# First attention of a two-layer stack on one core: keys and values as three-part products, heads paired across groups, query and output products between the pairs

## The chip, the core and the metric

The kernel runs on one core of a Trainium2 chip. The time is device time of one execution in microseconds (us). The engines are TensorE (PE; its weight loads are listed as PEld), VectorE (DVE), ScalarE (ACT), GpSimd (POOL) and SyncE (SP), which here only issues transfers.

## The reference

The model takes 16 meta tokens and 256 tokens of width 1024 through a pooling layer with a feed-forward network, then an attention layer with another one, and then through a second stack (gated branches and 32 routed experts), which the change leaves alone. What is touched is the first attention: 16 query heads of 64 in two groups of 8, each group with one key and value head, and a sliding window over blocks of 128.

```python
kv_in = rms_norm(hs, kv_norm)
k = (kv_in @ w_k + b_k).reshape(B, L, N_KV_HEADS, HEAD_DIM)
v = (kv_in @ w_v + b_v).reshape(B, L, N_KV_HEADS, HEAD_DIM)
...
q = (h @ w_q + b_q).reshape(B, L, N_KV_HEADS, GROUP, HEAD_DIM)
...
logits = jnp.einsum('bnqhgd,bnshd->bhgnqs', q, k_blk,
                    preferred_element_type=jnp.float32) * (HEAD_DIM ** -0.5)
...
m = jnp.maximum(logits.max(axis=-1, keepdims=True), sink)
p = jnp.exp(logits - m)
denom = p.sum(axis=-1, keepdims=True) + jnp.exp(sink - m)
probs = (p / denom).astype(v_blk.dtype)
o = jnp.einsum('bhgnqs,bnshd->bnqhgd', probs, v_blk)
...
return o @ w_o + b_o
```

## The kernel before

**Weights.** SP loads all weights of the dense layers in the order of `STREAM` (L55) into a ring of three slots. Tile number t goes to slot t % 3 and waits until the tile three places back is used up (`tile_done`, L310). For most weights that is when DVE has made the low part of both halves; for `w_kv`, which is not split, it is when the last product with it is done (`kv_psum` at 3). `w_kv` is tile 20, `w_q` 21 and 22, `w_o` 23 and 24, so the first tile of `w_o` follows `w_kv` in slot 2. SP works strictly in order.

**Three-part products.** A weight piece of 2048 columns is split into a rounded part (`wh`, by ACT, `split_hi`, L660) and a rest (`wl`, by DVE, `split_lo`, L668); activations likewise (`xh`, `xl`). A product is then three matmuls in a reduced 32-bit format (`mm3`, L1195): high with high, low with high, high with low. There are two buffers for split pieces and a third one for chosen pieces (`THIRD_FIRST`); a piece waits until the product of the piece before it in its buffer is done.

**First attention, before.** PE makes query columns 0 to 3 (L1233, L1239), then 4 to 7 (L1245, 24 matmuls each), turns the row of scales (L1250), and multiplies keys and values with plain 32-bit matmuls on `mix`, which POOL has filled (L598): keys twice, once for each group, laid out double so that both heads of a pair find them in their half of the partitions (L1258), and values by token (L1263). Then it waits for keys and values (L1266), and goes through 8 pairs of neighbouring heads: `scores`, `turn` (transposes of the weights) and `outputs` (L1301), with the scores two pairs ahead. After the last pair come the 8 output columns of `w_o`, 24 matmuls each. DVE, in its own fixed order, evicts query columns (L1880, L1881) with splits of `w_q` and `w_o` in between (the table `low` hangs the first piece of `w_o` behind query column 4), then keys (L1892) and values (L1899); per pair it adds the bias and takes the maximum (`logits`, L1912 to L1922), normalises (`shares`, L1929 to L1933) and makes the low part of the output (L1938). ACT does the exponentials (L811), the copies of what was turned (L821) and the high part (L826).

The bias table (`brev`) is loaded by SP after the first feed-forward network (L457), ahead of `w_o`.

## Time and profile before

| | us |
|---|---|
| three runs | 1093.58, 1090.06, 1093.87 |
| median | 1093.58 |
| span of the profiled execution | 1091.4 |
| PE busy in it | 980.6 |
| DVE, ACT, POOL busy | 535.7, 410.0, 167.7 |

The page gives the span, first to last instruction; the median of the runs is 2.2 us above it. The chain that ended last lies on PE for 84% of the span and on DVE for 7%; 1% is one transfer of `w_o`. Matmuls are pipelined, so a group's busy time overstates what each takes of the path; the distance between starts is the better price.

### The profile page before, as it was taken

The numbers are of one execution on the slowest core, as the hardware profiler recorded it, in microseconds if no ns is written. First come the engines' busy times: TensorE is split into PE (matmuls) and PEld (weight loads), VectorE is DVE, ScalarE is ACT, GpSimd is POOL, SyncE is SP. The second block draws the span as 40 slices with busy tenths as digits, with TensorE's granted clock in tenths as the row PEclk, the third lists the DMA queues.
The fourth block names the chain that finished last, engine by engine and source line by source line (L and its number), as shares of the span: only waits on it lengthen the run. The fifth ranks groups of instructions, "written<-read, shape, count | busy, mean of one in ns | idle before, by whom it ended". The sixth has DMA issues, their size and how long they took to land.

```text
span 1091.4 us, 16836 instructions
## 1 busy us (share of the span) xinstructions
PE 980.6 (90%) x6809; PEld 822.9 (75%) x6809; DVE 535.7 (49%) x976; ACT 410.0 (38%) x684; POOL 167.7 (15%) x224
## 2 busy tenths in 40 slices
PE   3799999998849999999987999979889999999866
PEld 2599999998737899999987999759644554455365
DVE  4655454347165655554435538674523334333254
ACT  3533333445047743344444456633211111111153
POOL 5432323015000333332101000000100000000000
PEclk8899999999959999999997999779799999999979
DMA  7325434454060425453562431028269999999601
GB/s 284 154 91 204 169 130 156 163 189 154 28 279 4 154 97 212 154 182 132 187 232 78 160 116 55 34 92 366 97 239 420 418 418 407 409 409 419 259 1 38
DMA packets 25646, 212.51 MB, mean 195 GB/s; under 512 B 2001, under 2 KB 5345, under 8 KB 5729
## 3 DMA queue, kind: packets, MB, share of 16 engines
q1 hardware_dynamic: 25568, 211.43, 50.0%
q8 instruction: 55, 0.90, 0.3%
q14 instruction: 23, 0.18, 0.0%
HBM read 210.35 MB, written 1.07 MB: 194 GB/s over the span
## 4 chain that ended last, share of the span: by engine, by line
PE 84%; DVE 7%; ACT 3%; issue 2%; POOL 2%; DMA 1%; POOLq 0%; DVEq 0%; ACTq 0%
PE ps L1195 48%; PE ps L1557 10%; PE ps L1571 5%; PE ps L1186 3%; PE ps L1580 3%; PE ps L1126 2%; PE ps L1529 2%; PE ps L1530 1%; DVE wl L668 1%; DVE mix L1685 1%; PE ps L1233 1%; DMA ring<-in_w_o 1%; PE ps L1134 1%; PE ps L1515 1%; PE ps L1258 1%
## 5 line engine op out<-in xcount | busy, mean ns | idle before, releaser
L668 DVE TENSOR_TENSOR wl<-ring,wh 128x2048 fp32r<-128x2048 f32 (+2 forms) x106 | 214.8, 2027 | 226.0 <-ACT wh L660 226.0
L660 ACT ACTIVATE wh<-ring 128x2048 fp32r<-128x2048 f32 (+2 forms) x106 | 179.6, 1697 | 304.1 <-PE ps L1195 268.6
L1195 PE MATMUL ps<-xh,wh 128*128 128x256 f32 (+3 forms) x712 | 203.5, 286 | 7.0 <-DVE xl L2227 7.0
L1195 PE MATMUL ps<-xh,wl 128*128 128x256 f32 (+3 forms) x712 | 201.9, 284 | 0.0
L1195 PE MATMUL ps<-xl,wh 128*128 128x256 f32 (+3 forms) x712 | 201.6, 283 | 0.0
L1195 PEld LDWEIGHTS ps<-xh,wh 128*128 128x128 f32 (+3 forms) x712 | 132.9, 187 | 8.5 <-issue 8.1
L1195 PEld LDWEIGHTS ps<-xh,wl 128*128 128x128 f32 (+3 forms) x712 | 132.9, 187 | 0.2
L1195 PEld LDWEIGHTS ps<-xl,wh 128*128 128x128 f32 (+3 forms) x712 | 132.8, 187 | 0.0
L1195 PE MATMUL ps<-acth,wh 128*128 128x272 f32 (+1 forms) x352 | 101.1, 287 | 0.0
L1195 PE MATMUL ps<-actl,wh 128*128 128x272 f32 (+1 forms) x352 | 100.0, 284 | 0.0
L1195 PE MATMUL ps<-acth,wl 128*128 128x272 f32 (+1 forms) x352 | 100.0, 284 | 0.0
L1195 PE MATMUL ps<-xhT,wl 128*128 128x272 f32 x320 | 92.6, 289 | 0.0
L1195 PE MATMUL ps<-xlT,wh 128*128 128x272 f32 x320 | 92.2, 288 | 0.0
L1195 PE MATMUL ps<-xhT,wh 128*128 128x272 f32 x320 | 91.3, 285 | 0.0
L530 POOL TENSOR_TENSOR sq<-sq 128x256 f32<-128x256 f32 (+1 forms) x15 | 20.9, 1397 | 445.7 <-ACT sq L644 445.7
L1195 PEld LDWEIGHTS ps<-acth,wh 128*128 128x128 f32 x352 | 66.5, 189 | 0.2
L1195 PEld LDWEIGHTS ps<-acth,wl 128*128 128x128 f32 x352 | 66.1, 188 | 0.2
L1195 PEld LDWEIGHTS ps<-actl,wh 128*128 128x128 f32 x352 | 66.2, 188 | 0.0
L2211 DVE TENSOR_TENSOR yl<-ps,yh 128x512 fp32r<-128x512 f32 x32 | 20.6, 686 | 91.4 <-ACT yh L1064 91.4
L539 POOL TENSOR_TENSOR mix<-mix 128x272 f32<-128x272 f32 (+1 forms) x44 | 36.7, 835 | 158.5 <-DVE mix L1719 142.6
L1557 PE MATMUL ps<-wring,xb_even 128*64 128x512 f32 x256 | 56.5, 593 | 5.0 <-issue 5.0
L1195 PEld LDWEIGHTS ps<-xhT,wh 128*128 128x128 f32 x320 | 60.4, 189 | 0.0
(382 smaller groups left out, 1778.5 us busy)
## 6 DMA issues: line engine op xcount, KB each, us to landing
wring<-in_w_eg SPq DMA_DIRECT2D x32, 2048.0 KB, 12.5
ring<-in_w_gu SPq DMA_DIRECT2D x22, 2048.0 KB, 8.0
wring<-in_w_ed SPq DMA_DIRECT2D x16, 2048.0 KB, 10.6
ring<-in_w_dn SPq DMA_DIRECT2D x16, 1408.0 KB, 5.9
ring<-in_w_z SPq DMA_DIRECT2D x7, 2048.0 KB, 7.7
ring<-in_w_out SPq DMA_DIRECT2D x4, 1152.0 KB, 5.1
ring<-in_w_q SPq DMA_DIRECT2D x2, 2048.0 KB, 7.7
ring<-in_w_o SPq DMA_DIRECT2D x2, 2048.0 KB, 10.1
```

Of the source, the lines that this page charges most:

```text
L530: pool.tensor_tensor(even, even, odd, ALU.add).then_inc(sem("sq_paired"), 1)
L539: pool.tensor_tensor(mix[:, 6 + j, 0:n], mix[:, 2 + j, 0:n], mix[:, 4 + j, 0:n], ALU.mult)\
L660: act.activation(high[:, 0:size], ring[:, slot, j * size:(j + 1) * size], ACT.Copy)\
L668: dve.tensor_tensor(low[:, 0:size], ring[:, slot, j * size:(j + 1) * size], high[:, 0:size].bitcast(F32), ALU.subtract).then_inc(sem("lo_d ...
L1126: pe.matmul(ps[:, 2 * j + g, 0:n], w[:, k * 256 + g * P:k * 256 + g * P + P], xa[:, k, 0:n], start=(k == 0 and part == 0), stop=False)
L1186: mm(ps[:, 6, 0:n], ones[0:rows, :], square_at(name, c + 1 - chunks)[0:rows, 0:n], start=(c < chunks), stop=(c == last))\
L1195: ins = mm(o, p, q, start=first and n == 0, stop=last and n == 2)
L1529: mm(out, h2h[:, k, at], select[:, k, :], start=(k == 0), stop=False)
L1557: ins = mm(ps[rows, 4, :], x[:, k, rows], chunk(b, c)[:, j, i * 512:(i + 1) * 512], start=(k == 0), stop=(k == KD - 1))
L1571: ins = mm(ps[rows, 6 + i, :], heT[:, k, rows], chunk(b, GU_CHUNKS)[:, j, k * D + i * 512:k * D + (i + 1) * 512], start=(k == 0), stop=(k ...
L1580: ins = mm(ps[:, c // 2, c % 2 * SEQ:(c % 2 + 1) * SEQ], y[:, c * P:(c + 1) * P], weights, start=False, stop=last and y is parts[-1], skip ...
L2211: dve.tensor_tensor(yl[:, i * 512:(i + 1) * 512], ps[:, 6 + i, :], yh[:, i * 512:(i + 1) * 512].bitcast(F32), ALU.subtract).then_inc(sem(" ...
```

## The change

`w_kv` leaves the ring. It is loaded early, right after the last tile of the first gate and up weights, into the free end of slot 2 (columns 4096 to 6143), only one copy of the keys and the values, in two transfers of 128 columns by 8 rows of each partition. It becomes a piece of its own in the order of splits, between the two tiles of `w_q`. `w_q` and `w_o` are tiles 20 to 23 now; each is loaded in four transfers that bring head u and head u+8 next to each other, so a pair is one head of each group and finds keys and values of its group in its half of the partitions. ACT and DVE make `xkh` and `xkl` in place of POOL's product; keys and values (as rows by channel) are three-part products, and the values are turned by three transposes. DVE evicts query columns 4 to 7 inside the loop over pairs. On PE, query column 4 stands ahead of the loop, 5 to 7 in its first three rounds, and the output products of columns 0 and 1 (`project`) in its last four. The outputs go to `att_h` and `att_l` instead of `xh` and `xl`, so that queries can still be made. The two score blocks of one head share a PSUM bank and stand one after the other; DVE goes by head as well. Later on, because every ring tile behind `w_kv` moves by one slot, the first loads of the experts go to slots 0, 1, 2, 3 instead of 1, 2, 3, 0, behind `w_out` tiles 1, 2, 2, 3, and the two tiles of `w_ple` are waited for at earlier counts. Two semaphores of the router are merged.

```diff
-STREAM = [("w_pool", 1, 2048), ("w_gu0", NF // 2, 4096), ("w_dn0", KD, FF), ("w_kv", 1, 3072),
+STREAM = [("w_pool", 1, 2048), ("w_gu0", NF // 2, 4096), ("w_dn0", KD, FF),
...
+SPLIT = [(_name, _p) for _name, _n, _ in STREAM if _name != "w_pool" for _p in range(2 * _n)]
+SPLIT.insert(SPLIT.index(("w_q", 2)), ("w_kv", 0))
+NUMBER = {_piece: _i for _i, _piece in enumerate(SPLIT)}
...
-        THIRD_FIRST = ("w_gu0", "w_q", "w_gu1", "w_z")
+        THIRD = (("w_gu0", 0), ("w_q", 0), ("w_q", 2), ("w_o", 1), ("w_gu1", 0), ("w_z", 0))
...
+                    if name == "w_q":
+                        src = a["w_q"][half, :, i * PIECE:(i + 1) * PIECE].rearrange("p (k c n) -> p k c n", k=KD, c=2)
+                        dst = ring[:, slot, 0:2 * PIECE].rearrange("p (c k h n) -> p h k c n", c=2, k=KD, h=2)
+                        for c in range(2):
+                            sp_.dma_start(dst[:, half, :, c, :], src[:, :, c, :]).then_inc(done, 16)
+                        continue
+                    for odd in range(2):
+                        src = a["w_o"][i, odd * HD:(odd + 1) * HD, :].rearrange("p (c h n) -> p c h n", c=2, h=2)
+                        dst = ring[half * HD:(half + 1) * HD, slot, 0:2 * PIECE].rearrange("p (c o n) -> p c o n", c=2, o=2)
+                        sp_.dma_start(dst[:, :, odd, :], src[:, :, half, :]).then_inc(done, 16)
...
+            kv = a["w_kv"].rearrange("a p (k n) -> (a p) k n", n=3 * P)
+            for j in range(2):
+                sp_.dma_start(wkv.rearrange("p (k n) -> p k n", n=2 * P)[:, :, j * P:(j + 1) * P],
+                              kv[:, :, HD + j * 3 * HD:HD + j * 3 * HD + P]).then_inc(sem("kv_loaded"), 16)
...
-            pool.wait_ge(sem("delta_ready"), 2 * KD)
-            for c in range(KD):
-                wait_hs(pool, 1, c)
-                pool.tensor_scalar(mix[:, c, :], hs[:, c, :], V("kv_norm", c), None, ALU.mult).then_inc(sem("kvin_ready"), 1)
...
-            split_hi(act, "w_q", *halves("w_q", 1, PIECE)[0])
+            kv_hi(act)
+            for c in range(KD):
+                act.activation(xkh[:, c, :], hs[:, c, :], ACT.Copy, scale=V("kv_norm", c)).then_inc(sem("xkh_ready"), 1)
             rsqrt(act, chain, "pre1", D, T)
-            split_hi(act, "w_q", *halves("w_q", 1, PIECE)[1])
-            for x in halves("w_o", 0, PIECE):
-                split_hi(act, "w_o", *x)
+            for x in halves("w_q", 1, PIECE):
+                split_hi(act, "w_q", *x)
+            split_hi(act, "w_o", *halves("w_o", 0, PIECE)[0])
...
+                if u in (1, 4):
+                    split_hi(act, "w_o", *(halves("w_o", 0, PIECE)[1] if u == 1 else halves("w_o", 1, PIECE)[0]))
             attended_high(HEAD_PAIRS - 1)
-            for k in range(NB):
-                split_hi(act, "w_o", *halves("w_o", 1, PIECE)[k])
-                for c in range(2 * k, 2 * k + 2):
-                    wo_out(act, c)
-            split_hi(act, "w_gu1", *halves("w_gu1", 0, PIECE)[0])
-            for c in range(4, KD):
+            for c in range(KD):
+                if c == 2:
+                    split_hi(act, "w_o", *halves("w_o", 1, PIECE)[1])
+                if c in (4, 6):
+                    split_hi(act, "w_gu1", *halves("w_gu1", 0, PIECE)[c // 2 - 2])
...
-            for c in range(4, KD):
-                pe.wait_ge(sem("lo_done"), FIRST_PIECE["w_q"] + c // 2 + 1)
-                pe.wait_ge(sem("q_ready"), c - 3)
-                for k in range(KD):
-                    ins = mm3(ps[:, c % 4, 0:SEQ], q_weights(c, k), (xh[:, k, 0:SEQ], xl[:, k, 0:SEQ]), k == 0, k == KD - 1)
-                ins.then_inc(sem("q_psum"), 1)
-            pe.wait_ge(sem("r_ready"), NORM["pre1"] + 1)
-            for j in range(NB + 1):
-                cols = slice(0, P) if j == 0 else slice(N_META + (j - 1) * P, N_META + j * P)
-                ins = pe.transpose(ps[:, 5, j * P:(j + 1) * P], r_of("pre1")[:, cols], ident)
-            ins.then_inc(sem("rcol_psum"), 1)
-            slot, rnd = tile_at(FIRST["w_kv"])
-            pe.wait_ge(sem(f"tile_ready{slot}"), 16 * (rnd + 1))
-            wkv = ring[:, slot, 0:3072].rearrange("p (k n) -> p k n", k=KD)
+            kvh, kvl = split_buffer("w_kv", 0, 0)
+            pe.wait_ge(sem("lo_done"), NUMBER["w_kv", 0] + 1)
             for j in range(2):
                 for k in range(KD):
-                    pe.wait_ge(sem("kvin_ready"), k + 1)
-                    ins = mm(ps[:, 4 + 3 * j, 0:T], wkv[:, k, j * P:(j + 1) * P], mix[:, k, :], start=(k == 0), stop=(k == KD - 1))
+                    pe.wait_ge(sem("xk_ready"), k + 1)
+                    at = slice(k * 2 * P + j * P, k * 2 * P + (j + 1) * P)
+                    ins = mm3(ps[:, 4 + j, 0:T], (kvh[:, at], kvl[:, at]), (xkh[:, k, :], xkl[:, k, :]), k == 0, k == KD - 1)
...
+            def query(c):
+
+                pe.wait_ge(sem("lo_done"), NUMBER["w_q", c // 2] + 1)
+                pe.wait_ge(sem("q_ready"), 4 if c < 6 else c - 1)
                 for k in range(KD):
-                    ins = mm(ps[0:cols.stop - cols.start, 6, j * P:(j + 1) * P], mix[:, k, cols], wkv[:, k, 2 * P:3 * P],
-                             start=(k == 0), stop=(k == KD - 1))
-            ins.then_inc(sem("kv_psum"), 1)
-            pe.wait_ge(sem("kT_ready"), 2)
-            pe.wait_ge(sem("v_ready"), NB + 1)
+                    ins = mm3(ps[:, 2 + c % 2, 0:SEQ], q_weights(c, k), (xh[:, k, 0:SEQ], xl[:, k, 0:SEQ]), k == 0, k == KD - 1)
...
             def scores(u):
-                for t in range(4):
-                    h, b = 2 * u + t % 2, t // 2
-                    rows = slice(t % 2 * HD, t % 2 * HD + HD)
-                    first, n = keys_of(t)
+                if u >= 4:
+                    pe.wait_ge(sem("q_ready"), u + 1)
+                for j in range(2):
+                    rows = slice(j * HD, j * HD + HD)
                     if u:
-                        pe.wait_ge(sem("lg_ready"), 4 * (u - 1) + t + 1)
-                    mm(ps[:, t, 0:n], qT[rows, u, b * P:(b + 1) * P], kT[rows, h // 8, first:first + n],
-                       start=True, stop=True).then_inc(sem("s_psum"), 1)
+                        pe.wait_ge(sem("lg_ready"), 4 * (u - 1) + 2 * j + 2)
+                    for t in (j, 2 + j):
+                        first, n = keys_of(t)
+                        ins = mm(score_bank(t)[:, 0:n], qT[rows, u, t // 2 * P:(t // 2 + 1) * P], kT[rows, first:first + n],
+                                 start=True, stop=True)
+                    ins.then_inc(sem("s_psum"), 1)
...
+            def project(c, k):
+
+                if k == 0:
+                    pe.wait_ge(sem("lo_done"), NUMBER["w_o", c // 2] + 1)
+                pe.wait_ge(sem("o_ready"), k + 1)
+                first = (k % 2 * 4 + k // 2) * 256 + c % 2 * P
+                at = slice(first, first + P)
+                return mm3(wo_bank(c), [x[:, at] for x in split_buffer("w_o", c // 4, c // 2 % 2)],
+                           (att_h[:, k, :], att_l[:, k, :]), k == 0, k == KD - 1)
+
+            pe.wait_ge(sem("kv_ready"), 1)
             scores(0)
             scores(1)
+            query(4)
+            values()
+            pe.wait_ge(sem("v_ready"), 2)
             for u in range(HEAD_PAIRS):
+                if u < 3:
+                    query(5 + u)
                 if u + 2 < HEAD_PAIRS:
                     scores(u + 2)
+                if u >= 4:
+                    for c in range(2):
+                        project(c, u - 4)
                 turn(u)
                 if u:
                     outputs(u - 1)
+            for k in range(4, 6):
+                for c in range(2):
+                    project(c, k)
             outputs(HEAD_PAIRS - 1)
-            for c in range(KD):
-                piece = FIRST_PIECE["w_o"] + c // 2
-                pe.wait_ge(sem("lo_done"), piece + 1)
-                if c >= 4:
-                    pe.wait_ge(sem("sq_ready"), SQ0["mixpost1"] + c - 3)
+            for c in range(2, 4):
+                for k in range(6):
+                    project(c, k)
+            for c in range(4):
+                for k in range(6, KD):
+                    ins = project(c, k)
+                ins.then_inc(sem("wo_psum"), 1)
+            for c in range(2):
+                sum_squares("mixpost1", c, SEQ)
+            for c in range(4, KD):
+                pe.wait_ge(sem("sq_ready"), SQ0["mixpost1"] + c - 3)
                 for k in range(KD):
-                    pe.wait_ge(sem("o_ready"), k + 1)
-                    at = slice(k * 256 + c % 2 * P, k * 256 + c % 2 * P + P)
-                    ins = mm3(ps[:, c % 4, 0:SEQ], [x[:, at] for x in split_buffer("w_o", c // 4, c // 2 % 2)],
-                              (xh[:, k, 0:SEQ], xl[:, k, 0:SEQ]), k == 0, k == KD - 1)
+                    ins = project(c, k)
                 ins.then_inc(sem("wo_psum"), 1)
-                if c >= 2:
-                    sum_squares("mixpost1", c - 2, SEQ)
+                sum_squares("mixpost1", c - 2, SEQ)
...
-            split_lo(dve, "w_q", *halves("w_q", 1, PIECE)[0])
+            kv_lo(dve)
+            for c in range(KD):
+                dve.wait_ge(sem("xkh_ready"), c + 1)
+                dve.scalar_tensor_tensor(xkl[:, c, :], hs[:, c, :], V("kv_norm", c), xkh[:, c, :].bitcast(F32),
+                                         ALU.mult, ALU.subtract).then_inc(sem("xk_ready"), 1)
...
-            low = {1: ("w_q", halves("w_q", 1, PIECE)[1]), 4: ("w_o", halves("w_o", 0, PIECE)[0])}
-            for c in range(KD):
...
+            def keyed():
+
+                dve.wait_ge(sem("kv_psum"), 1)
+                chain(dve.tensor_tensor(sq[:, 2, :], ps[:, 4, 0:T], r, ALU.mult))
+                dve.tensor_scalar(kT, sq[:, 2, :], key_bias, None, ALU.add).then_inc(sem("kv_ready"), 1)
+
+            def valued():
+
+                dve.wait_ge(sem("kv_psum"), 2)
+                dve.tensor_tensor(vT, ps[:, 5, 0:T], r, ALU.mult).then_inc(sem("kv_ready"), 1)
+
+            def by_token():
+
+                dve.wait_ge(sem("kv_psum"), 3)
+                b_v = R("b_v", P)
+                dve.tensor_tensor(vtok[0:N_META, 0, :], ps[0:N_META, 7, 0:P], b_v[0:N_META, :], ALU.add).then_inc(sem("v_ready"), 1)
+                dve.tensor_tensor(vtok[:, 1:NB + 1, :], ps[:, 7, P:3 * P].rearrange("p (b n) -> p b n", b=NB),
+                                  b_v.unsqueeze(1).to_broadcast([P, NB, P]), ALU.add).then_inc(sem("v_ready"), 1)
+
+            queried(0)
+            queried(1)
+            split_lo(dve, "w_q", *halves("w_q", 1, PIECE)[0])
+            queried(2)
+            queried(3)
+            keyed()
+            split_lo(dve, "w_q", *halves("w_q", 1, PIECE)[1])
             dve.wait_ge(sem("tables_loaded"), 64)
-            dve.wait_ge(sem("kv_psum"), 3)
-            b_v = R("b_v", P)
-            for j in range(NB + 1):
-                rows = slice(0, N_META if j == 0 else P)
-                dve.scalar_tensor_tensor(vtok[rows, j, :], ps[rows, 6, j * P:(j + 1) * P], small[rows, 128 + j:129 + j], b_v[rows, :],
-                                         ALU.mult, ALU.add).then_inc(sem("v_ready"), 1)
...
             logits(0)
+            valued()
             logits(1)
-            split_lo(dve, "w_o", *halves("w_o", 0, PIECE)[1])
+            by_token()
             for u in range(HEAD_PAIRS):
                 shares(u)
+                if u < 4:
+                    queried(4 + u)
                 if u + 2 < HEAD_PAIRS:
                     logits(u + 2)
                 if u >= 2:
                     attended_low(u - 2)
+                if u in (2, 3, 5):
+                    split_lo(dve, "w_o", *[*halves("w_o", 0, PIECE), halves("w_o", 1, PIECE)[0]][(2, 3, 5).index(u)])
             for u in range(HEAD_PAIRS - 2, HEAD_PAIRS):
                 attended_low(u)
-            for x in halves("w_o", 1, PIECE):
-                split_lo(dve, "w_o", *x)
+            split_lo(dve, "w_o", *halves("w_o", 1, PIECE)[1])
```

On SP, between the first feed-forward weights and the second ones, before:

```order
L424 DMA ring<-in_w_gu 128x4096 x2
L424 DMA ring<-in_w_dn 128x2816 x8
L424 DMA ring<-in_w_kv 128x3072
L424 DMA ring<-in_w_q 128x4096 x2
L457 DMA work<-bias_rows 128x16x256
L424 DMA ring<-in_w_o 128x4096 x2
```

and now:

```order
L461 DMA ring<-in_w_gu 128x4096 x2
L489 DMA ring<-in_w_kv 128x8x128 x2
L494 DMA small<-in_vec 64x4 x4
L461 DMA ring<-in_w_dn 128x2816 x8
L441 DMA ring<-in_w_q 128x8x128 x8
L502 DMA work<-bias_rows 128x16x256
L446 DMA ring<-in_w_o 64x2x1024 x8
```

The load of `w_kv` moved ahead of eight tiles; `w_o` still follows the bias table (`bias_rows`).

On DVE, from the low part of the query input to the first maximum of the scores (L1912 before, L2024 now, shown as ISA), before. The marks stand for further evictions of query columns and for the first piece of `w_o` among them:

```order
L1871 SCALAR_TENSOR_TENSOR xl<-hs,vec,xh 128x256 x8
L668 TENSOR_TENSOR wl<-ring,wh 128x2048
L1880 TENSOR_TENSOR sq<-ps,rstd 128x256
L1881 TENSOR_SCALAR work<-sq,vec 128x2x128
...
L668 TENSOR_TENSOR wl<-ring,wh 128x2048
...
L1892 TENSOR_TENSOR sq<-ps,rstd 128x272
L1893 TENSOR_SCALAR work<-sq,vec 128x272
...
L1899 SCALAR_TENSOR_TENSOR work<-ps,small,row 128x128 x2
L1912 ISA work,small<-ps,work 128x144
```

and now:

```order
L1968 SCALAR_TENSOR_TENSOR xl<-hs,vec,xh 128x256 x8
L733 TENSOR_TENSOR wl<-ring,wh 128x2048
L1973 SCALAR_TENSOR_TENSOR xkl<-hs,vec,xkh 128x272 x8
L1981 TENSOR_TENSOR sq<-ps,rstd 128x256
...
L720 TENSOR_TENSOR third_l<-ring,third_h 128x8x128 x2
...
L1989 TENSOR_TENSOR sq<-ps,rstd 128x272
L1990 TENSOR_SCALAR work<-sq,small 128x272
L720 TENSOR_TENSOR wl<-ring,wh 128x8x128 x2
L2024 ISA work,small<-ps,work 128x144
```

Before the first scores stand two splits of `w_q` and the one of `w_kv`, and none of `w_o`; the values (L1995) come behind the first pair's maxima.

On PE, from the last query column to the first scores, before:

```order
L1195 MATMUL ps<-xl,wh 128x256
L1250 MATMUL ps<-cst,rstd 128x128 x3
L1258 MATMUL ps<-mix,ring 128x272 x16
L1263 MATMUL ps<-ring,mix 16x128 x8
L1263 MATMUL ps<-ring,mix 128x128 x16
L1276 MATMUL ps<-work 128x144 x2
L1276 MATMUL ps<-work 128x256 x2
```

and now, from the last rest product of query column 3 (L1312) to the first query column between the pairs:

```order
L1312 MATMUL ps<-xl,wh 128x256 x16
L1268 MATMUL ps<-xkh,wh 128x272
L1268 MATMUL ps<-xkh,wl 128x272
L1268 MATMUL ps<-xkl,wh 128x272
...
L1348 MATMUL ps<-work 128x144
L1348 MATMUL ps<-work 128x256
L1348 MATMUL ps<-work 128x144
...
L1268 MATMUL ps<-xh,third_h 128x256
L1268 MATMUL ps<-xh,third_l 128x256
L1268 MATMUL ps<-xl,third_h 128x256
```

The scores stand directly behind 16 groups of three matmuls for keys and values, and the query columns 4 to 7 behind the scores.

## Rows read from the trace of the kernel before

**Rows 1.** The chain that ended last, in order of time: start, duration, what.

```profile
271.95 11.39 PE ps L1195 x96
283.67 7.33 PE ps L1258 x32
291.00 5.63 PE ps L1263 x48
296.65 7.82 DMA ring<-in_w_o
...
346.88 11.58 PE ps L1195 x96
...
371.65 0.71 PE ps L1186 x2
```

**Rows 2.** DVE in order of time, 259 to 313: start, duration, instruction, [idle before].

```profile
259.60 4.47 DVE L1871 SCALAR_TENSOR_TENSOR xl<-hs,vec,xh 128x256 fp32r<-128x256 f32 x8
263.99 2.28 DVE L668 TENSOR_TENSOR wl<-ring,wh 128x2048 fp32r<-128x2048 f32 x1
...
306.44 2.29 DVE L668 TENSOR_TENSOR wl<-ring,wh 128x2048 fp32r<-128x2048 f32 x1 [28.05 <-ACT wh L660]
308.65 0.42 DVE L1880 TENSOR_TENSOR sq<-ps,rstd 128x256 f32<-128x256 f32 x1
...
310.81 0.28 DVE L1888 COPY small<-ps 128x1 f32<-128x1 f32 x3
```

**Rows 3.** ACT in the same order, 268 to 308.

```profile
304.50 3.71 ACT L660 ACTIVATE wh<-ring 128x2048 fp32r<-128x2048 f32 x2 [30.59 <-DMA ring<-in_w_o]
```

**Rows 4.** SP's issues of transfers, 215 to 345.

```profile
227.94 0.33 SPq L424 DMA_DIRECT2D ring<-in_w_kv  x1
236.68 8.61 SPq L424 DMA_DIRECT2D ring<-in_w_q  x2
250.68 0.38 SPq L457 DMA_DIRECT2D work<-bias_rows  x1
296.65 0.81 SPq L424 DMA_DIRECT2D ring<-in_w_o  x2
```

**Rows 5.** PE in order of time, first pairs of heads.

```profile
313.57 5.49 PE L1276 MATMUL ps<-work 64*128 64x144 f32 x24 [16.95 <-DVE work L1899]
...
325.03 0.34 PE L1287 MATMUL ps<-cst,work 128*128 128x128 f32 x1
...
326.06 1.24 PE L1301 MATMUL ps<-mix,work 16*64 16x128 f32 x16
327.23 0.95 PE L1276 MATMUL ps<-work 64*128 64x144 f32 x8
```

**Rows 6.** DVE in order of time, inside the loop over pairs.

```profile
316.44 0.30 DVE L1912 CUSTOM_DVE_ANT_0 work<-ps,work 128x144 f32<-128x144 f32 x1
...
318.18 2.29 DVE L668 TENSOR_TENSOR wl<-ring,wh 128x2048 fp32r<-128x2048 f32 x1
...
330.24 1.03 DVE L1933 TENSOR_SCALAR work<-work,small 128x144 f32<-128x144 f32 x4
...
333.52 1.02 DVE L1933 TENSOR_SCALAR work<-work,small 128x144 f32<-128x144 f32 x4
```

**Rows 7.** POOL's sum of two squares behind the output products.

```profile
356.32 1.39 POOL L530 TENSOR_TENSOR sq<-sq 128x256 f32<-128x256 f32 x1 [85.47 <-ACT sq L644]
```

**Rows 8.** Stretches: length, busy PE, PEld, DVE, ACT, POOL, PE clock, DMA share, GB/s.

```profile
256.00:260.00 4.00, 3.95 (x20) 3.95 (x21) 3.93 (x9) 3.59 (x10) 2.17 (x3) 0.57 0.50 160
...
301.00:305.00 4.00, 0.00 (x0) 0.00 (x0) 0.00 (x0) 0.50 (x1) 0.00 (x0) 0.50 1.01 430
...
321.00:325.00 4.00, 3.40 (x16) 2.56 (x16) 3.86 (x24) 1.99 (x7) 0.00 (x0) 0.52 0.90 291
325.00:329.00 4.00, 4.00 (x42) 3.10 (x40) 3.69 (x22) 3.69 (x15) 0.00 (x0) 1.00 0.57 240
...
337.00:341.00 4.00, 2.84 (x31) 1.85 (x28) 3.86 (x22) 3.95 (x17) 0.00 (x0) 1.00 0.01 2
```

**Rows 9.** Transfers: KB each, median us from issue to landing.

```profile
ring<-in_w_q SPq DMA_DIRECT2D x2, 2048.0 KB, 7.7
...
work<-bias_rows SPq DMA_DIRECT2D x1, 2048.0 KB, 8.0
```

186 lines of the change are left out of this document (113 added, 73 removed).

## The prediction, made before the result was known

> **What bounds the kernel now.** I read the chain that ended last first, between 270 and 373 us, where the change lies. PE makes query columns 4 to 7 from 271.95 in 96 matmuls (11.39 us), then keys and values until 296.65; then the chain leaves PE for 7.82 us of a transfer of `w_o` [rows 1]. The orders of the other engines say why. SP issues `w_o` at 296.65, just when the last product with `w_kv` ends, since both use slot 2 [rows 4]. ACT has stood 30.59 us waiting for it [rows 3], DVE 28.05 us for ACT [rows 2], with the evictions of three query columns, keys and values behind that split. PE starts its scores at 313.57 after 16.95 us without work [rows 5], and at half clock: the granted clock is 0.50, that is 1.2 GHz, from 301, and at 1.00, 2.4 GHz, only from about 325 [rows 8]. In the loop over pairs PE is at 2.84 of 4 us busy while DVE has 3.86 [rows 8]: DVE sets the pace there, 3.28 us per pair (330.24 to 333.52) [rows 6]. From 346.88 PE is alone on the chain again, until the last sum of squares ends at 371.65 + 0.71 = 372.36 [rows 1]. Everything later follows that moment, so I compute the new time of it.
>
> **Prices.** A three-part matmul on 256 columns: 11.39 / 96 = 0.119 us, a group of three 0.357, a query column 2.85 [rows 1]; on 272 columns 0.119 x 272/256 = 0.126. An eviction of a query column on DVE: (310.81 - 308.65) / 3 = 0.72. A split of 2048 columns 2.29, a low part of a 256-column input 4.47 / 8 = 0.56, so 0.59 at 272 [rows 2]. `logits` of one pair: 318.18 - 316.44 = 1.74; the pace of 3.28 less these leaves 1.5 for `shares` and the low part, which I take as 1.3 and 0.33 (some 0.1 is given back by overlap) [rows 6]. `turn`: 326.06 - 325.03 = 1.03, of which I take 0.9 between other work; `outputs` 327.23 - 326.06 = 1.17 [rows 5].
>
> Scores of a pair take 0.95 us for 8 records, four of 144 and four of 256 columns [rows 5]. Keys show a plain 32-bit matmul of 272 columns at 7.33 / 32 = 0.229 us a record [rows 1]; at that rate 1600 columns are 1.35 us. So before, where the two heads (two halves of the partitions) alternate, they overlap. Now both blocks of one head stand together. I take 1.3 us, near the serial end, and 0.95 as the other bound: over three pairs on PE's path that is 1 us. The Trainium skill, TensorEngine Tiling (Array Packing), section Tiling Modes, says that different tiles of rows can load and multiply in parallel; the 0.95 us agree, and by it the new order loses what the old one had. By that rule alone the sum would be as mine; without it 1 us less.
>
> **Part by part.** Start: PE at 271.95, as before.
>
> 1. Keys and values: 48 x 0.126 = 6.0 us in place of 13.3, from the end of the query columns at 271.95 + 11.39 = 283.34 to 296.65 [rows 1]; PE is through at 278.0. DVE must have the low parts: it is free at 263.99, one split (2.3) and 8 x 0.59 bring it to 271.0, just ahead of PE's start and always ahead of its groups. ACT's extra 8 copies and one split fit into time in which it waits. POOL loses its 8 products, on nobody's path.
>
> 2. Before the first scores DVE has four query columns (2.9), two splits of `w_q`, each now two instructions on halves (2.4 each, my estimate from 2.29), and the keys (0.75): 271.0 + 8.5 = 279.5. PE has issued scores(0) by 279.3 and waits for the first head's maximum; scores(1) end near 281.5. Query column 4 to 284.4, three transposes (0.45) to 284.8; DVE adds the bias to the values by 285.5, so PE enters the loop at 285.6. The two waits cost 1.7 us in all.
>
> 3. Rounds 0 to 2 are PE's: a query column 2.85, scores 1.3, turn 0.9, in two of them outputs 1.17: 5.05 + 6.2 + 6.2 brings PE to 303.1. This is where three of four query columns are paid; they hide the DVE work of these rounds, not the other way round.
>
> 4. From there DVE sets the end again, since it now has query column 7 and three splits of `w_o` in the loop. Scores(4) end at 301.1, after the query column and the scores of round 2; the rest of their `logits`, a low part and the first split take it to 304.8; round 3 without that: 1.3 + 0.72 + 1.74 + 0.33 + 2.29 = 6.4; round 4: 3.4; round 5: 5.7; shares of round 6: 1.3. That is 321.6. PE has 2.6 us idle at most at a time, and its 8 groups of `w_o` in rounds 4 to 7 hide there.
>
> 5. The tail is PE's: half a turn 0.45, outputs 1.17, two groups 0.7, turn 0.9, outputs 1.17, four groups 1.4, outputs 1.17 = 7.0, to 328.6. Then 64 - 12 = 52 groups of `w_o` at 0.357 = 18.6, to 347.2. Sums of squares, 1.6. One new wait: the sums of columns 0 and 1 are queued ahead of column 4 and need two evictions on ACT and POOL's sum of 1.39 [rows 7], which start only when column 1 is closed, two columns earlier: 1.1 us. The last evictions, 0.7 us. Together 350.7; I say 351.
>
> The gain is 372.4 - 351 = 21.4 us. By terms: the stall 16.95, keys and values 7.3, some 7 of the 11.4 us of query columns hidden, the slow clock at the start of the loop some 3, 12 of 64 groups hidden (4.3); against that two waits (2.8), scores (some 1 on PE's path), and the splits and evictions which now lengthen the loop on DVE, some 13, where before they stood under the stall.
>
> **Transfers.** `w_q` goes from one transfer to four, of runs of 512 bytes. Its first tile now takes the place of `w_kv` at 227.94 [rows 4]. Its two splits take some 4.5 us, and PE is at work on the query columns by 256 (3.95 of 4 us busy [rows 8]), so the tile may take until 250: 22 us for 2048 KB. The bias table, also 2048 KB and in runs of 1 KB, took 8.0 us [rows 9]. Even half that rate, 16 us, is hidden. `w_o` is issued at about 251 behind the bias table and is wanted at 278; both tiles and the table are 6 MB, at 430 GB/s [rows 8] 15 us. Cost 0, bounds 0 and 10 us (a quarter of the rate for `w_q`). Later on, the new order of expert slots and the earlier `w_ple` change no wait that I find on the chain, 0.
>
> **Rivals.** (a) The clock. It fell to 0.50 in 301 to 305, after 4 us of idle PE, and averaged 0.57 in 256 to 260; it stayed at 1.00 with PE busy 2.84 of 4 us [rows 8]. My rounds 3 to 6 have PE busy about 60%, with pauses of 2.6 us, nearer to the latter. If it falls once and takes as long to come back as before (313.6 to 325), 11.4 us of PE's work run at half speed: 5.7 us, time 1078. (b) The slower side: the clock stays at 1.2 GHz through the whole loop, because no stretch is busy enough. Then queries too cost double: 11.4 more, and turns, scores, outputs and groups, some 30 us of work, take 60, of which DVE's time covers 10. That is 32 us over my figure, 1104. It decides at 43 us of half clock on PE's path, where the gain is gone. Against it: the query columns are dense. (c) The stall stays in another form: a piece of `w_o` or `w_q` comes late, to ACT first, and everything behind it in its fixed order waits. Only keys, values and hidden groups are gained, 7 to 10 us: 1084. (d) More: scores overlap as before, DVE's splits find cover, the two waits vanish: 4 us more, 1068.
>
> **How the numbers follow.** The profiled span of 1091.4 becomes 1070.0; the median stands 2.2 us above that span, so 1093.6 - 21.4 = 1072.2, and I say 1072. Chances: forecast (1069 to 1076) 0.64, (a) 0.15, (d) 0.11, (c) 0.06, (b) 0.04. The range from 1065 to 1083 takes in (d), with 3 us for the spread of the runs (1090.06 to 1093.87), and (a); it leaves out (b), (c) and the worst of the splits. About 0.5%, 5.5 us, is what a measurement of this kernel can tell from no change. Faster by more than that: 0.94; within: 0.03; slower: 0.03.
>
> **What would show it.** Right: `w_o` issued near 251, no idle time of ACT on it, no PE pause over 3 us between 272 and 351, keys and values in 6 us, PE paused before turns in rounds 3 to 6 with DVE as releaser, the clock at 1.00 throughout, the last sum of squares near 351 and everything later 21 us earlier with unchanged distances. Wrong: `w_q` landing after 250, a clock of 0.5 in the loop, pauses for DVE in the first three rounds, or a second feed-forward network that starts as much earlier as I say while the end does not.

## The result, and the profile after

| | before | after |
|---|---|---|
| runs | 1093.58, 1090.06, 1093.87, 1090.24 | 1068.52, 1069.75, 1070.99, 1063.74 |
| median | 1091.91 | 1069.13 |
| span of the profiled execution | 1091.4 | 1066.8 |
| PE busy in it | 980.6 | 974.7 |

The change made the kernel faster: 22.8 us by the medians in the table (1069.13 / 1091.91 = 0.979), 24.6 us by the two profiled spans, and 26.0 us in a repeat below (1067.64 against 1093.65). The ratio estimated from all runs is 0.9752, with a 95% interval of 0.9714 to 0.9791; on 1091.91 us that would be 27 us less, 1064.8 us. The forecast was 1072, a gain of 21.4 us, with a range of 1065 to 1083.

The attention is compared in each trace from the start of the first rest product of the query to the end of the last sum of squares. Before, that is 268.15 to 372.36, 104.2 us (the start is PE's row of L1239, the end is in [rows 1]). After, it is 265.02 to 347.19 + 0.71 = 347.90, 82.9 us. **The change gives 21.3 us there.** The other 3.1 us were there before the attention began. They come and go: that start lies at 264.84 to 268.02 us in the eleven traces with the new layout, and at 268.15 and 268.26 in the two with the old one. Behind the attention, 719.0 us were left before and 718.9 after, so nothing is given back. That these two agree to 0.1 us is chance: in the repeat it is 714.8, and in the seven further variants without added matmuls 712.2 to 717.1. To compare moments with the forecast, add 3.1 us to those of after.

First the chain that ended last, beside [rows 1] (start, duration, what):

```profile
265.02 1.93 PE ps L1312 x16
...
267.03 2.02 ACT third_h L710 x2
...
269.07 2.36 DVE third_l L720 x2
...
276.68 1.51 PE ps L1348 x8
278.19 3.04 PE ps L1268 x24
...
299.30 2.20 DVE wl L720
...
303.71 2.10 PE ps L1372 x16
305.81 1.64 PE ps L1348 x8
...
314.71 2.20 DVE wl L720
...
325.88 5.24 PE ps L1268 x42
...
347.19 0.71 PE ps L1259 x2
```

The transfer of 7.82 us is gone from it. In its place the chain leaves PE for more than 5 us three times: once before the loop, for the halves of the second tile of `w_q` on ACT and DVE, and twice in the loop, for DVE's work on a pair with a piece of `w_o` in it. PE alone, in order of time, shows keys and values (first and last record, 268.69 to 274.62) and what it waits for, beside [rows 5]:

```profile
268.69 0.29 PE L1268 MATMUL ps<-xkh,wh 128*128 128x272 f32 x1
...
274.62 0.29 PE L1268 MATMUL ps<-xkl,wh 128*128 128x272 f32 x1
274.84 0.95 PE L1348 MATMUL ps<-work 64*128 64x144 f32 x8
276.68 1.51 PE L1348 MATMUL ps<-work 64*128 64x144 f32 x8 [0.89 <-DVE small L2024]
...
282.27 0.39 PE L1268 MATMUL ps<-xh,third_h 128*128 128x256 f32 x1 [0.70 <-DVE work L2002]
...
302.43 0.33 PE L1360 MATMUL ps<-cst,work 128*128 128x128 f32 x1 [2.22 <-DVE work L2045]
...
317.84 0.33 PE L1360 MATMUL ps<-cst,work 128*128 128x128 f32 x1 [1.44 <-DVE work L2045]
```

Where a single pause was 16.95 us long, four are now 5.25 us together (0.89, 0.70, 2.22 and 1.44). ACT (first row) and DVE (the others), beside [rows 2, 3]:

```profile
275.01 1.91 ACT L710 ACTIVATE wh<-ring 128x2048 fp32r<-128x2048 f32 x1 [4.07 <-PE ps L1268]
```

```profile
256.90 3.77 DVE L1968 SCALAR_TENSOR_TENSOR xl<-hs,vec,xh 128x256 fp32r<-128x256 f32 x8
260.71 2.29 DVE L733 TENSOR_TENSOR wl<-ring,wh 128x2048 fp32r<-128x2048 f32 x1
262.92 3.38 DVE L1973 SCALAR_TENSOR_TENSOR xkl<-hs,vec,xkh 128x272 fp32r<-128x272 f32 x8
...
269.07 2.36 DVE L720 TENSOR_TENSOR third_l<-ring,third_h 128x1024 fp32r<-128x1024 f32 x2 [1.28 <-ACT third_h L710]
```

ACT's split of `w_o` now waits 4.07 us for PE (the buffer is in use by keys and values) instead of 30.59 for a transfer. SP's issues beside [rows 4], then the transfers by kind (KB each, median us to landing) beside [rows 9]:

```profile
225.25 12.83 SPq L441 DMA_DIRECT2D ring<-in_w_q  x8
247.99 0.37 SPq L502 DMA_DIRECT2D work<-bias_rows  x1
248.40 6.13 SPq L446 DMA_DIRECT2D ring<-in_w_o  x8
275.92 0.35 SPq L461 DMA_DIRECT2D ring<-in_w_gu  x1
```

```profile
ring<-in_w_q SPq DMA_DIRECT2D x8, 512.0 KB, 6.2
ring<-in_w_o SPq DMA_DIRECT2D x8, 512.0 KB, 16.0
...
work<-bias_rows SPq DMA_DIRECT2D x1, 2048.0 KB, 8.2
```

And the stretches beside [rows 8], with the clock (columns as there):

```profile
264.00:268.00 4.00, 4.00 (x32) 3.84 (x31) 3.72 (x10) 1.80 (x4) 0.00 (x0) 1.00 1.03 216
...
298.00:302.00 4.00, 2.21 (x26) 1.38 (x24) 3.86 (x12) 3.10 (x12) 0.00 (x0) 1.00 0.00 0
302.00:306.00 4.00, 3.57 (x26) 2.55 (x28) 3.90 (x19) 1.34 (x3) 0.00 (x0) 0.66 0.00 0
306.00:310.00 4.00, 4.00 (x20) 3.35 (x21) 3.93 (x14) 2.19 (x11) 0.00 (x0) 0.50 0.42 86
310.00:314.00 4.00, 4.00 (x41) 3.16 (x40) 3.48 (x21) 3.41 (x5) 0.00 (x0) 0.99 0.95 406
```

Two things here were not in the forecast: the clock falls to 1.2 GHz behind the pause of 2.22 us, until about 310, and `w_o` arrives at only 216 GB/s with the transfer engines full.

### The profile page after: what moved, and what is told of

Read it like the earlier page. It is cut to its first block, busy times and chain, and to the rows that moved or that the text cites. A ratio compares the mean times of both kernels' runs of the same rounds, so it can differ in the third digit from the quotient of the medians.

```text
span 1066.8 us, 16807 instructions
## 1 busy us (share of the span) xinstructions
PE 974.7 (91%) x6776; PEld 819.1 (77%) x6777; DVE 540.2 (51%) x986; ACT 416.1 (39%) x697; POOL 155.6 (15%) x216
## 4 chain that ended last, share of the span: by engine, by line
PE 85%; DVE 7%; ACT 3%; issue 2%; POOL 2%; DMA 0%; POOLq 0%; DVEq 0%; ACTq 0%
PE ps L1268 49%; PE ps L1651 11%; PE ps L1665 5%; PE ps L1259 3%; PE ps L1674 3%; PE ps L1623 2%; PE ps L1199 2%; DVE wl L720 2%; PE ps L1624 1%; DVE mix L1779 1%; PE ps L1306 1%; PE ps L1372 1%; PE ps L1207 1%; PE ps L1609 1%; PE ps L1592 1%
## 5 line engine op out<-in xcount | busy, mean ns | idle before, releaser
L720 DVE TENSOR_TENSOR wl<-ring,wh 128x2048 fp32r<-128x2048 f32 (+3 forms) x106 | 210.3, 1987 | 193.9 <-ACT wh L710 193.9
L710 ACT ACTIVATE wh<-ring 128x2048 fp32r<-128x2048 f32 (+3 forms) x106 | 176.1, 1665 | 267.2 <-PE ps L1268 265.2
L1268 PE MATMUL ps<-xh,wh 128*128 128x256 f32 (+3 forms) x632 | 180.5, 286 | 6.4 <-DVE xl L2343 6.4
L1268 PE MATMUL ps<-xh,wl 128*128 128x256 f32 (+3 forms) x632 | 179.0, 283 | 0.0
L1268 PE MATMUL ps<-xl,wh 128*128 128x256 f32 (+3 forms) x632 | 178.8, 283 | 0.0
L1268 PEld LDWEIGHTS ps<-xh,wh 128*128 128x128 f32 (+3 forms) x632 | 117.6, 186 | 7.8 <-issue 7.5
L1268 PEld LDWEIGHTS ps<-xh,wl 128*128 128x128 f32 (+3 forms) x632 | 117.6, 186 | 0.1
L1268 PEld LDWEIGHTS ps<-xl,wh 128*128 128x128 f32 (+3 forms) x632 | 117.5, 186 | 0.0
L1651 PE MATMUL ps<-wring,xb_even 128*64 128x512 f32 x256 | 60.0, 607 | 4.1 <-issue 4.0
L1268 PEld LDWEIGHTS ps<-xlT,wh 128*128 128x128 f32 x320 | 60.1, 188 | 0.0
```

The costliest lines, as they stand in the source:

```text
L710: ins = act.activation(to, src, ACT.Copy)
L720: ins = dve.tensor_tensor(to, src, h.bitcast(F32), ALU.subtract)
L1268: ins = mm(o, p, q, start=first and n == 0, stop=last and n == 2)
L1651: ins = mm(ps[rows, 4, :], x[:, k, rows], chunk(b, c)[:, j, i * 512:(i + 1) * 512], start=(k == 0), stop=(k == KD - 1))
```

## The experiments

All spans of attention below are from the same two marks. The kernels were timed beside the kernel before, whose median was 1093.65, 1092.98 and 1092.61 in the three series.

**The changed kernel again** gives the spread of the marks.

> The changed kernel once more, unedited. Theory: of the 24.6 us between the two spans 21.3 lie between the end of the first rest products of the query and the last sum of squares of the attention (104.2 us before, 82.9 after), and 2.7 us were there already before 57 us, where only the moment at which TensorE went to 2.4 GHz differs. If that is chance, the stretch up to the first group of three matmuls (62.96 in the trace before, 60.27 in the one after) moves by about 3 us in this run too, while the 82.9 us stay within 1 us. If it belongs to the change, it stays near 60.3.

Measured: 1067.64, ratio 0.9763 (0.9695 to 0.9832), attention 266.79 to 349.69, 82.9 again. The clock falls at the same place: 0.50 in 306 to 310. The first group of three matmuls starts at 62.05, between the 62.96 of before and the 60.27 of the first trace, so the early difference is in the main spread, as the theory of chance says, if by 1.8 and not 3 us. The attention repeats to 0.1 us, while the total moves by some us. The small effects below are read from the attention.

**The stall alone.** The kernel before, with only the splits of the first tile of `w_o` moved, so that the evictions and the scores no longer stand behind them:

```diff
-            for x in halves("w_o", 0, PIECE):
-                split_hi(act, "w_o", *x)
...
+                if u in (4, 5):
+                    split_hi(act, "w_o", *halves("w_o", 0, PIECE)[u - 4])
...
-            low = {1: ("w_q", halves("w_q", 1, PIECE)[1]), 4: ("w_o", halves("w_o", 0, PIECE)[0])}
+            low = {1: ("w_q", halves("w_q", 1, PIECE)[1])}
...
-            split_lo(dve, "w_o", *halves("w_o", 0, PIECE)[1])
...
+                if u >= 6:
+                    split_lo(dve, "w_o", *halves("w_o", 0, PIECE)[u - 6])
```

> The kernel before, with w_kv in its ring slot, plain products, neighbouring heads; only the splits of the first two pieces of w_o stand elsewhere: ACT's behind pairs 4 and 5, DVE's behind pairs 6 and 7. Theory: the stall of 16.95 us was one of order, not of the ring slot. Then the scores start near 299 in place of 313.6, at full clock, and the time falls by 17 to 20 us, to 0.982 to 0.985 of before. Rival: the transfer of w_o itself is the bound (it still lands at 304.5) or DVE's splits only move into the loop: under 10 us.

Measured: 1083.34, ratio 0.9891 (0.9855 to 0.9926); attention 93.6, a gain of 10.6 and not 17 to 20. The scores start at 297.80 instead of 313.57, 15.8 us earlier, as expected. But the product with `w_o`, which follows the loop, starts 12.3 us earlier (346.88 to 334.56), and then runs partly at half clock (three stretches of its trace, then its chain):

```profile
326.00:330.00 4.00, 1.99 (x12) 1.57 (x8) 2.99 (x9) 2.82 (x10) 0.00 (x0) 0.50 0.00 0
330.00:334.00 4.00, 4.00 (x32) 2.72 (x32) 1.56 (x2) 1.14 (x3) 0.00 (x0) 0.50 0.50 131
334.00:338.00 4.00, 4.00 (x22) 3.67 (x19) 0.42 (x1) 0.38 (x1) 0.00 (x0) 0.50 0.91 389
```

```profile
334.56 13.41 PE ps L1195 x96
```

The same 96 matmuls took 11.58 us before. So of the 15.8 us, 3.5 are lost again in the loop and 1.7 behind it. The stall was not empty: two splits stood under it, and they come back in the loop. The order alone gives half of the change's gain in the attention; no data layout is needed for it.

**The form of keys and values.** In the changed kernel, plain 32-bit products on the high part of the input, 16 matmuls in place of 48; the low part of the input is left out.

```diff
-                    ins = mm3(ps[:, 4 + j, 0:T], (kvh[:, at], kvl[:, at]), (xkh[:, k, :], xkl[:, k, :]), k == 0, k == KD - 1)
+                    ins = mm(ps[:, 4 + j, 0:T], wkv[:, at], xkh[:, k, :].bitcast(F32), start=(k == 0), stop=(k == KD - 1))
```

> The changed kernel with keys and values as plain 32-bit products on the high part of the input alone (its low part is left out), in 16 matmuls of 272 columns in place of 48 three-part ones; everything else, and so the one copy of the keys, as changed. A plain 32-bit matmul of 272 columns leaves two records, 0.229 us each in the kernel before, so 16 of them take 7.3 us where the three-part products take 6.0: theory 1, of the 7.3 us gained on keys and values, 6.0 come from making the keys once instead of twice and the values by channel instead of by token, and only 1.3 from the three-part form; PE's path gets 1.3 us longer until the first scores, which DVE then makes up for in part (it waits 0): attention +0 to +1.3 us, 83 to 84.2. Theory 2, the three-part form carries the gain: the 16 matmuls take 10 us or more, attention +3 us or more.

Measured, the step on its chain, and after it the same step's length in the changed kernel from the rows above, 274.84 - 268.69 = 6.15 us:

```profile
271.58 7.33 PE ps L1320 x32
```

The attention takes 84.1 us (267.78 to 351.91), 1.2 more; one execution, 1065.8. Theory 1 holds: the price per record is that of before (0.229 us), and of the gain on keys and values only about 1.2 us is the three-part form; 6 us come from computing keys once, with the values as rows.

**Queries ahead of the scores.** All four late query columns, and their evictions, stand before the loop again:

```diff
+            for c in range(4, KD):
+                query(c)
...
-            query(4)
...
-                if u < 3:
-                    query(5 + u)
```

> The changed kernel with the four query columns 4 to 7 all ahead of the first scores (and DVE's evictions of them ahead of the first maxima), none in the loop. Theory of the prediction: some 7 of their 11.4 us were hidden, so the attention is 6 to 8 us longer than 82.9, at full clock; more (8 to 12) if without them the rounds have pauses long enough to bring the clock down. Rival: DVE sets the whole loop, and the loop gets shorter by what is taken out: 0 to 4 us.

Measured: 1069.93, ratio 0.9778 (0.9745 to 0.9811), attention 86.5, so 3.6 more. This is the rival's range. Moving queries into the loop is worth at most half of the 7 us that I gave it. A likely reason is that PE has to do them in either place, while in the changed kernel DVE waits meanwhile (its rows show 2.02, 0.99 and 2.46 us before the first maxima of the first three rounds). The clock is in the 3.6 us too: it was low from about 293.5 to 300 and again from about 324 to 327, which the theory had left out. This trace also holds a comparison that the changed kernel does not offer, the same pause of 2.22 us:

```profile
308.33 0.33 PE L1360 MATMUL ps<-cst,work 128*128 128x128 f32 x1 [2.22 <-DVE work L2046]
```

```profile
298.00:302.00 4.00, 4.00 (x32) 2.92 (x32) 3.33 (x20) 3.54 (x12) 0.00 (x0) 0.71 0.00 0
302.00:306.00 4.00, 4.00 (x44) 2.79 (x40) 3.42 (x16) 3.80 (x10) 0.00 (x0) 1.00 0.02 4
306.00:310.00 4.00, 1.78 (x18) 1.29 (x18) 3.90 (x16) 4.00 (x17) 0.00 (x0) 1.00 0.00 0
310.00:314.00 4.00, 2.60 (x28) 1.90 (x25) 3.90 (x11) 2.57 (x11) 0.00 (x0) 1.00 0.18 29
```

Here the clock did not fall, although PE was busy for only 1.78 of the 4 us.

**No output products between pairs.** The 12 groups go back behind the loop:

```diff
-                if u >= 4:
-                    for c in range(2):
-                        project(c, u - 4)
...
-            for k in range(4, 6):
-                for c in range(2):
-                    project(c, k)
             outputs(HEAD_PAIRS - 1)
-            for c in range(2, 4):
+            for c in range(4):
```

> The changed kernel, with all output products of columns 0 and 1 behind the last pair (12 groups of three matmuls leave the loop). Theory: 12 x 0.357 = 4.3 us go back onto PE's path, less what they cost in the loop's tail, where 4 of them stood on the path already: 2.5 to 4.5 us longer. Rival: nothing was hidden, the loop becomes shorter by as much: 0 to 1 us.

Measured: 1072.86, ratio 0.9809 (0.9742 to 0.9875), attention 90.1: 7.2 us more, where 12 groups are 4.3 and I had expected 2.5 to 4.5. The remaining 2.9 us go with the clock (three stretches):

```profile
306.00:310.00 4.00, 2.92 (x20) 1.86 (x18) 3.86 (x11) 2.25 (x10) 0.00 (x0) 0.50 0.00 0
...
318.00:322.00 4.00, 2.70 (x20) 1.97 (x19) 3.93 (x9) 3.38 (x14) 0.00 (x0) 0.50 0.00 0
322.00:326.00 4.00, 4.00 (x26) 3.01 (x25) 1.58 (x8) 1.84 (x6) 0.00 (x0) 0.50 0.02 4
```

It falls behind the same pause and then stays at 1.2 GHz until 329, some 23 us and not 7. So without the groups of `w_o` between the pairs the clock stays low for the later half of the loop, which is rival (b) for that half. What in the groups brings it back is not shown. It is not that long matmuls are needed: with the queries first, the clock was low from about 293.5 and at 1.00 again from 301, and in between PE did scores, turns and outputs only.

**Scores in one half.** Both heads of a pair read the same half of the partitions, so no pair can overlap; the second head's scores are those of the wrong rows.

```diff
-                    rows = slice(j * HD, j * HD + HD)
+                    rows = slice(0, HD)
```

> The changed kernel with the scores of both heads of a pair computed from the first half of the partitions (the output is not the attention's; only where the operands lie differs). The 8 records of one pair took 0.89 us, not the 1.3 of the prediction. Theory: they still overlap although the blocks of a head stand together, since the other half can start while the first is busy: with one half alone a pair takes 1.2 to 1.4 us. Rival: matmuls with 64 rows are simply cheaper than the price worked out from 128 rows: still 0.9 us.

The first row is of this kernel, the second of the changed one, scores of one pair on PE in the loop:

```profile
288.40 1.62 PE L1348 MATMUL ps<-work 64*128 64x144 f32 x8
```

```profile
311.59 0.95 PE L1348 MATMUL ps<-work 64*128 64x144 f32 x8
```

On the chain they are 1.55 and 0.89 to 0.94 us. So the overlap of the two halves is still there when a head's two blocks stand together, and the price that I took, 1.3, near the serial end, was wrong: it is the 0.95 of before. The Trainium skill, TensorEngine Tiling (Array Packing), section Tiling Modes, says that tiles of different rows can load and multiply in parallel. The trace agrees, and shows that they need not alternate matmul by matmul; that the new order loses the overlap was my inference, not the page's. The total did not move (1068.59, two executions), and the attention only by 1 us (83.9). The clock stayed at 1.00 from 262 to 350 here, so keeping it up in that place is worth little by itself; the longer scores are in the same figure, so it is no clean test.

**POOL back at work.** POOL makes its eight products again, into columns that nobody reads.

```diff
+            for c in range(KD):
+                wait_hs(pool, 1, c)
...
+                pool.tensor_scalar(work[:, 11424:11696], hs[:, c, :], V("kv_norm", c), None, ALU.mult).then_inc(sem("kvin_ready"), 1)
```

> The changed kernel with POOL's eight products of the key input back, written to a place that nobody reads. In the kernel before, DVE's eight low parts took 4.47 us while POOL did these products, in the changed kernel 3.77, and eight of 272 columns 3.38. Theory: POOL's products slow DVE: with them back the 256-column group takes 4.3 to 4.6 us and the 272-column one 4.5 or more, and the time changes by less than 1 us, since DVE waits for ACT behind it. Rival: the duration belongs to the operands: 3.8 and 3.4 as now.

```profile
258.32 4.16 DVE L1975 SCALAR_TENSOR_TENSOR xl<-hs,vec,xh 128x256 fp32r<-128x256 f32 x8
```

The eight low parts take 4.16 us, against 3.76 or 3.77 in all ten traces of the new layout without these products, and 4.47 before; those of keys and values 3.83 against 3.38. Two executions, 1066.08. That lies between theory and rival: 0.39 of the 0.70 us won on the first rows is POOL's leaving, the rest is not explained. The Trainium skill, GPSIMD Engine Reference, section Key points, says that GpSimd shares its SBUF interfaces with VectorE and contends with its instructions that have two SBUF inputs; these rows are such ones, and agree.

**Splits under cover.** The three low parts of `w_o` leave rounds 2, 3 and 5 of the loop: one stands where DVE waits before the loop (1.98 us for the turned values), one in round 2 ahead of the maxima, where it waits for scores, one after the last pair.

```diff
+            split_lo(dve, "w_o", *halves("w_o", 0, PIECE)[0])
...
+                if u == 2:
+                    split_lo(dve, "w_o", *halves("w_o", 0, PIECE)[1])
...
-                if u in (2, 3, 5):
-                    split_lo(dve, "w_o", *[*halves("w_o", 0, PIECE), halves("w_o", 1, PIECE)[0]][(2, 3, 5).index(u)])
+                if u == 7:
+                    split_lo(dve, "w_o", *halves("w_o", 1, PIECE)[0])
```

> The changed kernel, with DVE's three splits of w_o in the loop moved to where DVE waited: the first between the maxima of pair 1 and the bias of the values, the second ahead of the maxima of pair 4, the third behind pair 7. Theory: from round 2 on DVE set the end, and the pause of 2.2 us before the turns of round 3 brought TensorE to 1.2 GHz for 302 to 310. Then both go: the clock stays at 1.00 in the loop, and the attention is 3.5 to 7 us shorter than 82.9. Rival: PE set the end in the later rounds anyway: under 1.5 us.

Measured: **1062.63**, ratio 0.972 (0.9652 to 0.9788); attention 77.4, 5.5 us less than the changed kernel, as expected. The pause before the turn of round 3 is 0.44 us instead of 2.22, and the clock does not fall; it is 1.00 from 270 to 334:

```profile
302.00:306.00 4.00, 3.56 (x36) 2.56 (x35) 3.83 (x21) 3.55 (x14) 0.00 (x0) 1.00 1.01 430
306.00:310.00 4.00, 4.00 (x40) 3.09 (x40) 3.86 (x22) 3.44 (x11) 0.00 (x0) 1.00 0.04 16
310.00:314.00 4.00, 3.59 (x36) 2.87 (x34) 3.06 (x18) 4.00 (x13) 0.00 (x0) 1.00 0.02 6
```

Its attention is the shortest so far. By the total it is 5.0 us below the changed kernel timed in the same series (1067.64), with intervals of the ratios that overlap.

**More under cover.** The same with a further move of the third piece of `w_o` (the text below calls it the fourth), on ACT from pair 4 to pair 7 and on DVE behind the last low part of the output, and with the two waiting sums of squares put behind output column 4:

```diff
-                if u in (1, 4):
+                if u in (1, 7):
...
-            for c in range(2):
-                sum_squares("mixpost1", c, SEQ)
...
+                if c == 4:
+                    for d in range(2):
+                        sum_squares("mixpost1", d, SEQ)
...
             for u in range(HEAD_PAIRS - 2, HEAD_PAIRS):
                 attended_low(u)
+            split_lo(dve, "w_o", *halves("w_o", 1, PIECE)[0])
```

> e6_covered with three further edits: ACT's high parts of the fourth piece of w_o go from pair 4 to pair 7, DVE's low parts of it behind the last low part of the output, and the sums of squares of output columns 0 and 1 stand behind column 4 of PE's order, no longer ahead of it. Theory 1 (after e6_covered nothing of DVE or ACT in the loop is on PE's path any more but what a pair itself needs; the wait for POOL's sum was 0.41 us): attention 76.5 to 77.5 us against 77.4, total within 1.5 us of e6_covered, 1061 to 1063. Theory 2 (the pieces still lengthen rounds 4 to 7): attention 74 to 76, total 1059 to 1061. If the columns of the fourth piece come too late for PE: attention 78 to 81.

Measured: 1063.65, ratio 0.9736 (0.9697 to 0.9775), attention 75.9 (267.81 to 343.76). That is 1.4 less than with the first three moves, at the upper end of theory 2; the total can't tell it from them, and which of the edits gave it was not tested.

**The pause filled.** Five unread plain matmuls on PE ahead of the turn of round 3, to keep the clock up:

```diff
+                if u == 3:
+                    pe.wait_ge(sem("q_ready"), 7)
+                    for _ in range(5):
+                        mm(ps[:, 2, 0:SEQ], ones[:, :], r_of("pre1")[:, N_META:], start=True, stop=True)
```

> The changed kernel with five matmuls added whose result nobody reads (ones times the scales, plain 32-bit, 256 columns, some 2.1 us) in TensorE's pause before the turns of round 3; DVE's order is untouched. Theory: the pause, not the amount of work, costs. The granted clock, 0.50 in 306 to 310 of the changed kernel, stays at 1.00, and the attention (82.9 us from the first rest product to the last sum of squares) gets 2 to 3.5 us shorter although PE does more. Rival: DVE sets the end there, the slow clock costs nothing: 82.9 or up to 0.5 more.

Measured: 1084.24 (1075.38 to 1091.23), ratio 0.9883 (0.9829 to 0.9936), but attention 83.4, so the 2 to 3.5 us of the theory did not come. The pause moved on behind the filled stretch and the clock fell there (0.58 in 310 to 314); what a clock at 1.00 would be worth was therefore not tested. The 15 us lay elsewhere, and since that could have been a disturbance, it was run again:

> The changed kernel with five unread plain matmuls of 256 columns on PE ahead of the turn of round 3, as in e7_filled, measured once more. e7_filled was 15 us slower than the changed kernel, but until 350 us its trace was within 1 us of it; the loss lay between 800 and 1000 us, in the stretch of the experts, where its transfers ran at 349 to 405 GB/s for stretches of 20 us, against 417 to 421 in the changed kernel. If that is a matter of those executions (another load on the memory), the experts' stretch is back at 419 GB/s and the kernel at 1067 to 1071 us. If it is the edit, the rate is again under 405 and the time 1080 to 1088 us. In both cases the attention (first rest product of the query to the last sum of squares) takes 82.5 to 84.5 us.

Measured: 1078.24 (1073.73 to 1082.37), ratio 0.9847 (0.9793 to 0.9902); attention 85.5, above the 82.5 to 84.5 expected, the clock again at 0.50, in 322 to 326. The total misses both expected ranges; two executions took 1074 and two 1082 us. Most of the loss is again in the stretch of the experts, far behind the edit. Its share of transfer time is as high as ever, the rate is not (first row: this kernel; second: the changed one, of which all stretches of 20 us from 800 to 980 show 417 to 421 GB/s):

```profile
880.00:920.00 40.00, 38.25 (x209) 19.30 (x210) 13.58 (x39) 6.04 (x13) 0.00 (x0) 1.00 0.99 398
```

```profile
880.00:900.00 20.00, 20.00 (x108) 10.13 (x105) 8.35 (x29) 2.81 (x6) 0.00 (x0) 1.00 1.01 421
```

PE then waits between groups, mostly 1.3 to 2.2 us at a time, put down to nothing in the profile. But this is no mark of the added matmuls. The two traces of the old layout show the same, the kernel before (first row, from its chain) and the one with only the splits moved (second):

```profile
885.19 1.44 issue
```

```profile
880.00:900.00 20.00, 20.00 (x106) 9.25 (x104) 5.44 (x19) 2.46 (x5) 0.00 (x0) 0.97 0.92 357
```

Before, four such pauses stand between 854 and 949 us, of 1.27 to 1.44 us, at 403 to 419 GB/s; the other trace has four between 814 and 942, up to 3.41 us. The nine traces of the new layout without added matmuls have none over 0.3 us between 800 and 960. So four of thirteen traces show it, of three different kernels. Whether the five matmuls bring it about, or whether it comes with single executions, is open; no run here tells.

## Why the prediction was right, and where it was not

The sign, the course and the gain inside the attention (21.3 us against 21.4) were right. Two steps failed. The first is "the clock at 1.00 throughout": TensorE went to 1.2 GHz in the loop, from about 303.5 to 310, which I had named as a sign of being wrong; all that it is seen to cost is 0.35 us of waiting on DVE. The second is the one that moved the total: "Start: PE at 271.95, as before" with "everything later follows that moment". I put everything outside the attention at nothing. The runs gained 22.8 to 27 us in all, so 1.5 to 6 us lie outside it: the attention starts 3.1 us earlier in the first trace and 1.4 in the repeat, and behind it the repeat is 4.2 us shorter (714.8 against 719.0). Part of this is spread between executions; the two traces of the old layout have slow stretches of the experts' transfers, as shown above. Whether the new order of the experts' slots has a part in it stays open, since only two traces of the old layout are there to compare with.

Inside the attention the forecast stands step by step beside the trace, whose moments are raised by 3.1 us:

| step of the prediction | forecast | trace + 3.1 |
|---|---|---|
| 2, first maxima on DVE | 279.5 | 279.1 |
| 2, second scores end | 281.5 | 281.3 |
| 2, PE enters the loop | 285.6 | 285.4 |
| 3, end of PE's stretch, round 2 | 303.1 | 303.3 |
| 4, last shares of DVE that bind | 321.6 | 321.4 |
| 5, loop over | 328.6 | 329.0 |
| 5, last sum of squares | 351 | 351.0 |

In the profiled execution the span was 3.2 us below the 1070.0 forecast for it, and 3.1 of that are the start of the attention. "Unchanged distances" behind the attention held there (719.0 and 718.9), by chance, as the repeat shows.

**Right in the mechanism.** The stall went because ACT no longer waits for a transfer; rounds 0 to 2 are PE's, and from there to the start of the tail DVE is never idle for more than 0.35 us while it sets the end; PE's longest pause is 2.22 us where I said 2.6.

**Right by compensation.** Steps 2 to 4 met their moments with some terms wrong. Under Prices and in step 3, a pair's scores cost 0.89 to 0.94, not 1.3, and an input's low part 0.42, not 0.59. The time that DVE won so, 1.28 us before the `w_q` pieces, it spent waiting: the piece of `w_q` that takes the third buffer can be split by ACT only when PE has finished with the first piece (1.12 us of ACT's wait for L1312, on the chain). I had read only DVE's load there, and not the buffer. In step 5 the wait for POOL's sum was 0.41 us and not 1.1.

**Wrong: the transfers.** "6 MB, at 430 GB/s 15 us" was a mis-sized term, though it cost nothing. The bias table took its 8.2 us, but the 4 MB of `w_o` behind it ran at 212 to 219 GB/s with the transfer engines full (the row 264 to 268 above), 19.4 us in place of 9.8. Its pieces write 64 partitions each. They are also smaller and in shorter runs than before (512 KB, 4 KB), but that is not it: `w_q`, in 512 KB and runs of 512 bytes to all 128 partitions, ran at 290 to 322 GB/s (236 to 242), and the bias table in runs of 1 KB at 348 to 364 (250 to 256 before). The last one landed 21.9 us after its issue at 253.9, at 275.8, so the whole took 28 us. The cost was 0 as forecast, since the first tile, which ACT took up at 275.01, was through about 9 us before (247.99 + 8.2 + 9.7 = 265.9, my estimate from these rows), and the second is split only from 311.98. The Trainium skill, DMA: Bandwidth & Descriptors, section Rules for kernel authors, asks for 128 partitions for the highest bandwidth, and says that transfers to the two halves of the partitions serialise. The trace agrees: pieces of both halves were on the way together, and in sum they ran at 216 against 430 GB/s.

**Wrong: the clock at 1.00 throughout.** Rival (a), with 0.15, came true as a mechanism, not as a price. The clock fell once, behind the pause of 2.22 us, in the repeat too, and stayed low until about 310. In these 7 us outputs took 2.10 instead of 1.17 us and scores 1.64 instead of 0.9. But DVE had a split of its own there (2.28 us from 305.42), so PE's delay made it wait only 0.35 us (its row at 312.68). I had charged the rival with 5.7 us, all of it on the path. The error was to take one stretch of 2.84 busy that kept its clock [rows 8] for a rule. The runs give none: with the queries first, the clock stayed up behind the same pause of 2.22 us and with less work around it.

**Wrong: the terms of the gain, taken apart.** In my list the stall was worth 16.95, queries 7, keys and values 7.3, groups 4.3. Taken one by one, on the chip: 10.6 (in the kernel before), 3.6, of keys and values 1.2 by form, and 7.2 for the groups. The clock has a part in the 3.6 and the 7.2. The list came to the right sum with 13 us of splits and evictions booked against it in another line. No single term of it can be carried elsewhere as a price. That some of these 13 us were a matter of place, and not of need, is shown by the kernels with splits under cover, 5.5 and 6.9 us faster in the attention; step 4 named the splits as what lengthens the loop, and I did not ask where else DVE stood idle.

## What to carry to other kernels

When an engine is idle behind a transfer, look what stands in its queue that needs no transfer; moving that was worth half of this large change's gain in the attention, in some ten lines. When work is moved into a loop, put each split where its engine already waits: the waits of DVE in rounds 0 to 2 stood in the profile. Work for PE between short matmuls can buy more than its own time: here 12 groups of 4.3 us were worth 7.2, and the clock was low for 7 us with them and 23 us without. A stretch of one trace does not tell whether the clock will stay up; count what each level would cost on the path. And before a difference far from an edit is put down to it, look for it in the traces of the other kernels, the one before too.

## What the hardware showed that I had not expected

- Transfers that write 64 partitions each ran at half rate, 212 to 219 GB/s, with the share of transfer time at 1.03; those of `w_o` to all 128 at 430 before.
- The clock fell behind a pause of 2.22 us in the changed kernel and its repeat, and stayed at 1.00 behind one of 2.22 us with the queries first. Once down, it was back after 7 us in these two, after 7 us with only scores, turns and outputs in between where the queries stood first, and after some 23 us where the groups of `w_o` were taken out.
- Two half-height matmul sequences overlap (0.95 against 1.62 us for 8 records) though one head's blocks stand together.
- Between 820 and 960 us the experts' transfers ran at 416 to 421 GB/s in nine traces. In the other four (both with the added matmuls, and both of the old layout) single stretches fell to between 351 and 403 GB/s, with pauses of PE between groups. Not explained.
